# Roots as logarithm and exponential on ScalarE, spreads, scores and gate parts moved, one low split on VectorE

## What is computed

```
# first block
h = rms_norm(x, norm1_g); proj = h @ w_in            # q, k, v, glu_a, glu_b
q, k = rms_norm(q per head), rms_norm(k per head)    # root over 64 columns
log_one_minus = where(mask, log_sigmoid(-z), 0)      # z = q.k / 8, 8 heads
weights = where(mask, exp(log_sigmoid(z) + reversed exclusive cumsum(log_one_minus)), 0)
c = causal_depthwise_conv(glu_a * sigmoid(glu_b), 31 taps)
c = silu(layer_norm(c))                              # root over 512 channels
x = x + concat(weights @ v, c) @ w_out               # then a gated feed-forward
# second block
branch a: differential attention, 4 heads, o = rms_norm(o) * 0.8     # root per head
branch b: compressed + selected + window attention, 8 heads, gated
x = x + (sigmoid gates * branches) @ w_out           # gates = h @ w (16 tiles)
x = x + cross_attention(x, mem); x = rms_norm(x + peer(x))   # 16384 experts
```

## Time and profile before

| | |
|---|---|
| median of 3 runs | 2403.93 us (2403.37 to 2405.93) |
| profiled execution | 2401.27 us, span 2399.5 us, mean clock 0.997 |
| busy share | PE 98%, DVE 74%, ACT 47%, POOL 57% |
| chain that ended last | PE 88%, DVE 5%, POOL 2%, DMA 2%, ACT 2% |

### The profile page before, as it was taken

One profiled execution on the slowest core, in us unless ns is written; L12 is line 12 of the kernel. 1 busy time (PEld: TensorE's weight loads), 2 busy tenths in 40 slices (PEclk: granted clock), 3 DMA queues, 4 the chain that ended last, 5 costly groups with the idle time before them and its releaser, 6 DMA issues.

```text
span 2399.5 us, 32826 instructions
## 1 busy us (share of the span) xinstructions
PE 2345.9 (98%) x11991; PEld 1989.8 (83%) x11991; DVE 1770.4 (74%) x2989; ACT 1120.0 (47%) x2163; POOL 1370.6 (57%) x698
## 2 busy tenths in 40 slices
PE   8999999999999999999999999999999999999998
PEld 7866888888886666888889999999999888888887
DVE  4986674253236766564899978999983799999998
ACT  4356322223214556335543448888883433333333
POOL 3423455454432211433535777777777889888884
PEclk9999999999999999999999999999999999999999
DMA  4201222322421101222215687999999899999995
GB/s 161 88 18 36 100 93 81 112 88 87 178 89 53 38 34 54 105 106 95 99 62 161 226 288 261 354 351 351 354 353 383 323 360 378 376 364 358 361 356 210
DMA packets 152500, 476.60 MB, mean 199 GB/s; under 512 B 14768, under 2 KB 47920, under 8 KB 142000
## 3 DMA queue, kind: packets, MB, share of 16 engines
q1 hardware_dynamic: 115504, 340.69, 39.3%
q0 software_dynamic: 36864, 134.23, 15.6%
HBM read 422.44 MB, written 52.43 MB: 198 GB/s over the span
## 4 chain that ended last, share of the span: by engine, by line
PE 88%; DVE 5%; POOL 2%; DMA 2%; ACT 2%; issue 1%; SPq 0%; ACTq 0%; DVEq 0%; POOLq 0%
PE bank_pair L2401 22%; PE bank_pair L286 17%; PE bank_pair L288 17%; PE bank_pair L287 17%; PE bank_pair L2370 2%; PE bank_pair L775 1%; PE bank_pair L1448 1%; PE bank_pair L1485 1%; POOL u_lo L2074 1%; PE bank_pair L1501 1%; PE bank_pair L297 1%; PE bank_pair L1457 1%; PE bank_pair L298 1%; DVE stage L2545 1%; POOL w_lo L255 1%
## 5 line engine op out<-in xcount | busy, mean ns | idle before, releaser
L255 POOL TENSOR_TENSOR w_lo<-w_raw,w_hi 128x2048 fp32r<-128x2048 f32 (+3 forms) x94 | 408.9, 4350 | 573.3 <-ACT w_hi L250 573.3
L2074 POOL TENSOR_TENSOR u_lo<-u_raw,u_hi 128x1024 fp32r<-128x1024 f32 x128 | 315.8, 2468 | 168.7 <-ACT u_hi L2070 168.1
L286 PE MATMUL bank_pair<-uh,u_lo 128*128 128x384 f32 x1024 | 345.7, 338 | 6.6 <-POOL u_lo L2074 5.9
L287 PE MATMUL bank_pair<-ul,u_hi 128*128 128x384 f32 x1024 | 343.3, 335 | 0.0
L288 PE MATMUL bank_pair<-uh,u_hi 128*128 128x384 f32 x1024 | 343.2, 335 | 0.0
L2130 POOL TENSOR_TENSOR v_lo<-v_raw,v_hi 128x1024 fp32r<-128x1024 f32 x128 | 308.8, 2413 | 44.1 <-ACT v_hi L2126 42.8
L250 ACT ACTIVATE w_hi<-w_raw 128x2048 fp32r<-128x2048 f32 (+3 forms) x95 | 171.5, 1805 | 288.0 <-PE bank_pair L288 280.1
L2597 DVE TENSOR_TENSOR h_raw<-h_raw,g_in 128x384 f32<-128x384 f32 x128 | 261.0, 2039 | 49.5 <-DMA h_raw<-h_scratch 49.5
L2126 ACT ACTIVATE v_hi<-v_raw 128x1024 fp32r<-128x1024 f32 x128 | 135.8, 1061 | 288.3 <-PE bank_pair L2401 217.4
L286 PE MATMUL bank_pair<-xh,w_lo 128*128 128x512 f32 x624 | 246.0, 394 | 5.1 <-DVE sig L1737 2.1
L287 PE MATMUL bank_pair<-xl,w_hi 128*128 128x512 f32 x624 | 243.6, 390 | 0.0
(11 more groups left out here) (460 smaller groups left out, 5247.7 us busy)
## 6 DMA issues: line engine op xcount, KB each, us to landing
w_raw<-w_small SPq DMA_DIRECT2D x77, 1024.0 KB, 4.8
u_raw<-expert_u SPq DMA_DIRECT2D x128, 512.0 KB, 5.9
v_raw<-expert_v SPq DMA_DIRECT2D x128, 512.0 KB, 7.5
h_scratch<-h_act SPq DMA_DIRECT2D x128, 192.0 KB, 4.5
g_scratch<-stage SPq DMA_DIRECT2D x24, 1024.0 KB, 8.1
g_in<-g_scratch SPq DMA_DIRECT2D x16, 1536.0 KB, 11.7
h_raw<-h_scratch SPq DMA_DIRECT2D x128, 192.0 KB, 6.6
w_raw<-w_small SPq DMA_DIRECT2D x8, 768.0 KB, 4.2
```

The lines of the kernel that those rows point to most:

```text
L255: pool.tensor_tensor(wl[g % 2][:, :n], raw[g % 2][:, :n], wh[g % 2][:, :n].bitcast(F32), ALU.subtract).then_inc(sem("lo_done"), 1)
L286: pe.matmul(out, al, bh, start=(k == 0), stop=False)
L287: pe.matmul(out, ah, bl, start=False, stop=False)
L2074: pool.tensor_tensor(u_lo[c % 2][:, :, :], u_raw[c % 4][:, :, :], u_hi[c % 2][:, :, :].bitcast(F32), ALU.subtract)\
```

## The change

- The low split of weight block 1 goes from GpSimd to VectorE. The spread of the first norm goes from behind tile 3 of `in_fm` to before the sixth k (k = 5) of tile 3.
- The three places with Sqrt on ScalarE and a reciprocal of 128x512 on VectorE (q and k, layer norm, four heads of the second block) become Ln and Exp with scale -0.5, both on ScalarE.
- In `in_v` the spreads are behind tiles 2, 3, 4, 6, `scores(0)` behind tile 5, and `softplus(0)` stands before the last four convolution steps.
- Four gates parts go from steps 44 to 47 to steps 48 to 50. The high split of the next gates block goes behind the squares, and `gates_out(10)` before the eight subtractions.

```diff
-        def linear_pe(pe, name, pairs_of, ncols, ready=None, between=None, behind=(), sliced=False):
+        def linear_pe(pe, name, pairs_of, ncols, ready=None, between=None, behind=(), sliced=False, inside=()):
...
+                        hook = ready if first else dict(inside).get(n) if first_step else None
+                        products(pe, out, pairs_of(s % 2, m), hook).then_inc(sem("lin_done"), 1)
...
-        CONV_A, CONV_V = 6, (2, 0, 0, 2, 2, 2, 4, 4)
+        CONV_A, CONV_V = 6, (2, 2, 0, 0, 2, 2, 4, 4)
-        SPREAD_TILES = (3, 4, 5, 6)
+        SPREAD_TILES = (2, 3, 4, 6)
...
+            act.preload_act_table_set("natural_log_exp_and_others")
             act.wait_ge(sem("qk_sum"), 1)
-            act.activation(std16[:, :], att_bank[0][:, :], ACT.Sqrt, bias=eps[:, 0:1], scale=1.0 / HD)\
+            act.activation(std16[:, :], att_bank[0][:, :], ACT.Ln, bias=eps[:, 0:1], scale=1.0 / HD)\
                .then_inc(sem("qk_std"), 1)
-            act.preload_act_table_set("natural_log_exp_and_others")
+            act.wait_ge(sem("qk_std"), 1)
+            act.activation(rstd16[:, :], std16[:, :], ACT.Exp, scale=-0.5).then_inc(sem("qk_rstd"), 1)
...
-            act.activation(ln_std[:, :], att_bank[3][:, :], ACT.Sqrt, bias=eps[:, 0:1], scale=1.0 / CW)\
+            act.activation(ln_std[:, :], att_bank[3][:, :], ACT.Ln, bias=eps[:, 0:1], scale=1.0 / CW)\
                .then_inc(sem("ln_std"), 1)
+            act.wait_ge(sem("ln_std"), 1)
+            act.activation(ln_rstd[:, :], ln_std[:, :], ACT.Exp, scale=-0.5).then_inc(sem("ln_std"), 1)
...
-            pool.wait_ge(sem("lo_done"), 3)
-            for b in range(1, second):
+            pool.wait_ge(sem("lo_done"), 4)
+            for b in range(2, second):
...
+            def spread_at_fifth(k):
+                if k == 5:
+                    norm_spread("n1", norm_diag1, S)(pe)
+
             linear_pe(pe, "in_fm", weights_first("in_fm", xh, xl), S, follow_lo(pe, "n1"),
-                      behind=(None, first_sum, norm_spread("n1", norm_diag1, S)), sliced=True)
+                      behind=(None, first_sum), sliced=True, inside=((3, spread_at_fifth),))
...
-                    pe.wait_ge(sem("qk_rstd"), 1)
+                    pe.wait_ge(sem("qk_rstd"), 2)
...
-            in_v_behind[6] = first_scores
+            in_v_behind[5] = first_scores
+            in_v_behind[6] = last_spreads
...
+            split_lo(dve, 1)
...
-                                    row_in_group[:, 0:4].unsqueeze(2).to_broadcast([P, 4, HD]))
-                    dve.wait_ge(sem("qk_std"), 1)
-                    dve.reciprocal(rstd16[:, :], std16[:, :]).then_inc(sem("qk_rstd"), 1)
+                                    row_in_group[:, 0:4].unsqueeze(2).to_broadcast([P, 4, HD])).then_inc(sem("qk_rstd"), 1)
...
+                if n == 7:
+                    softplus(0)
...
-            dve.wait_ge(sem("ln_std"), 1)
-            chain.link(dve.reciprocal(ln_rstd[:, :], ln_std[:, :]))
+            dve.wait_ge(sem("ln_std"), 2)
...
+        HELD = (1, 1, 1, 1, 2, 1, 1)
...
+            if u < N_A:
+                return range(u, u + 1)
+            first = N_A + 2 * min(u - N_A, NU - 4 - N_A) + sum(HELD[:max(0, u - (NU - 4))])
+            return range(first, first + (2 if u < NU - 4 else HELD[u - (NU - 4)]))
...
+            for n in gates_ended(NU + 2):
+                split_hi(act, GATES["block"] + n // 2 + 2)
+            act.preload_act_table_set("natural_log_exp_and_others")
             for h in range(DA_H):
                 act.wait_ge(sem("sub_sum"), h + 1)
-                act.activation(sub_std[:, h, :], att_bank[h][:, :], ACT.Sqrt, bias=eps[:, 0:1], scale=1.0 / P)\
+                act.activation(sub_std[:, h, :], att_bank[h][:, :], ACT.Ln, bias=eps[:, 0:1], scale=1.0 / P)\
                    .then_inc(sem("sub_std"), 1)
+            for h in range(DA_H):
+                act.wait_ge(sem("sub_std"), h + 1)
+                act.activation(sub_std[:, h, :], sub_std[:, h, :], ACT.Exp, scale=-0.5).then_inc(sem("sub_std"), 1)
...
-            wait(pe, ("at_max", 2 * NU), ("bank_free", 4 + GATES["tile"] + EARLY))
+            wait(pe, ("at_max", 2 * NU))
             for h in range(DA_H):
+                if h >= 2:
+                    pe.wait_ge(sem("bank_free"), 4 + GATES["tile"] + EARLY - 2 + h - 1)
...
-                dve.wait_ge(sem("sub_std"), h + 1)
-                chain.link(dve.reciprocal(sub_std[:, h, :], sub_std[:, h, :]))
+                dve.wait_ge(sem("sub_std"), DA_H + h + 1)
                 dve.scalar_tensor_tensor(out=oab[:, h, :], in0=oab[:, h, :], scalar=subln_g[:, 0:1],
                                          in1=sub_std[:, h, :], op0=ALU.mult, op1=ALU.mult).then_inc(sem("sub_y"), 1)
+                if h == DA_H - 1:
+                    gates_out(EARLY)
```

More of the change, by code:

```diff
@@ L327, in step @@
                         first = first_step and n == 0
-                        products(pe, out, pairs_of(s % 2, m), ready if first else None).then_inc(sem("lin_done"), 1)
+                        hook = ready if first else dict(inside).get(n) if first_step else None
+                        products(pe, out, pairs_of(s % 2, m), hook).then_inc(sem("lin_done"), 1)
                         if between:
@@ L821, in first_scores, with last_spreads @@
                 scores(0)
+            def last_spreads(pe):
                 pe.wait_ge(sem("bank_free"), 4 + LAYER["in_v"]["tile"] + 6)
@@ L921, in block1_dve, with softplus @@
                 conv += CONV_A
+            def softplus(h):
+                dve.wait_ge(sem("st_ln"), h + 1)
+                if h >= 2:
+                    dve.wait_ge(sem("st_tail"), h - 1)
+                for b, (off, w) in enumerate(PIECES):
+                    ins = dve.scalar_tensor_tensor(out=soft[h % 2][:, off:off + w], in0=head_banks(h)[b][:, :w], scalar=0.0,
+                                                   in1=ln1[:, off:off + w], op0=ALU.max, op1=ALU.add)
+                ins.then_inc(sem("st_soft"), 1)
             for n in range(8):
@@ L940, in block1_dve @@
                 conv += CONV_V[n]
-            def softplus(h):
-                dve.wait_ge(sem("st_ln"), h + 1)
-                if h >= 2:
-                    dve.wait_ge(sem("st_tail"), h - 1)
-                for b, (off, w) in enumerate(PIECES):
-                    ins = dve.scalar_tensor_tensor(out=soft[h % 2][:, off:off + w], in0=head_banks(h)[b][:, :w], scalar=0.0,
-                                                   in1=ln1[:, off:off + w], op0=ALU.max, op1=ALU.add)
-                ins.then_inc(sem("st_soft"), 1)
-            softplus(0)
             softplus(1)
@@ L1160, in gates_bank @@
             return att_bank[2 + n % 2] if n < EARLY else lin_bank[n % 4]
+        HELD = (1, 1, 1, 1, 2, 1, 1)
         def gates_parts(u):
-            return range(u, u + 1) if u < N_A else range(N_A + 2 * (u - N_A), N_A + 2 * (u - N_A) + 2)
+            if u < N_A:
+                return range(u, u + 1)
+            first = N_A + 2 * min(u - N_A, NU - 4 - N_A) + sum(HELD[:max(0, u - (NU - 4))])
+            return range(first, first + (2 if u < NU - 4 else HELD[u - (NU - 4)]))
         def gates_ended(u):
-            return [q // KD for q in gates_parts(u) if q % KD == KD - 1] if u < NU else []
-        assert N_A == 2 * KD and gates_parts(NU - 1)[-1] == EARLY * KD - 1
+            return [q // KD for q in gates_parts(u) if q % KD == KD - 1] if u < NU + 3 else []
+        assert N_A == 2 * KD and gates_parts(NU + 2)[-1] == EARLY * KD - 1
         def score_bank(u, c):
@@ L1513, in block2_pe @@
                         scores(s)
-                    gates_part(gates_parts(s)[0])
+                gates_part(gates_parts(s)[0])
                 if s in (1, 2):
@@ L1518, in block2_pe @@
                     transposes(s - 2)
-                if s < NU:
-                    for q in gates_parts(s)[1:]:
-                        gates_part(q)
+                for q in gates_parts(s)[1:]:
+                    gates_part(q)
                 if s >= 3:
                     values(s - 3)
-            wait(pe, ("at_max", 2 * NU), ("bank_free", 4 + GATES["tile"] + EARLY))
+            wait(pe, ("at_max", 2 * NU))
             for h in range(DA_H):
+                if h >= 2:
+                    pe.wait_ge(sem("bank_free"), 4 + GATES["tile"] + EARLY - 2 + h - 1)
                 pe.wait_ge(sem("sub_sq"), h + 1)
@@ L1765, in block2_dve @@
                    .then_inc(sem("oab_lo"), 1)
-            for n in range(EARLY, 2 * KD):
+            for n in range(EARLY + 1, 2 * KD):
                 gates_out(n)
```

## The result

The changed kernel takes 2388.72 us (median of 4 runs, 2388.01 to 2389.31), the kernel before in the same comparison 2404.93 (2403.37 to 2408.59). The ratio is 0.9934, 95% interval 0.9921 to 0.9946. The forecast was 2389.3, range 2385.5 to 2395, 14.6 us under 2403.93. The profiled execution took 2389.23 us with a span of 2387.5, that is 12.0 us less than the profiled one of before, where the medians differ by 16.2. The 4 us between the two lie in how single executions scatter: the profiled one of before is 3.7 us under its median, the profiled one of the changed kernel 0.5 above its own.

The account below looks back on a forecast made before the run. TensorE, busy 98% of the span, was taken as the bound, with 53.6 us idle to win from. Terms 3.2 + 4.3 + 2.4 + 0.9 + 3.8 = 14.6 us off 2403.93 gave 2389.3 us, range 2385.5 to 2395.

Parts of the forecast that it names:

- Start: in_fm: waits of 1.56 and 1.51 us at tiles 2 and 4 go, 3.2 us (bounds 2.4 and 3.4).
- Heads: in_v and first heads: earlier `softplus(0)` removes the tails' wait and low clock, scores(2) 4.3 us earlier (2.7 to 5.5).
- Layer norm: out1: Ln and Exp remove waits of 1.40 and 0.75 us and two restarts, 2.4 us (bounds 1.2 and 2.6).
- Rival 4: Layer norm: table switch costs ScalarE its load twice, Silu 1.28 us later, time 2390.0 us; chance 0.10.
- Drain: End of second block's attention: moved gates parts fill the 0.63 us idle, 0.9 us (bounds -0.5 and 1.8).
- Gates tile 14: Second block: wait of 2.05 us for `gates_out(10)` and low clock behind it go, 3.8 us (bounds 2.0 and 3.9).
- Clock: Behind the first tails' wait and gates tile 14, the lower granted clock goes, 1.7 us each.
- Rival 1: Clock or handovers give less: without both clock terms 11.2 us gained, 2392.7 us; chance 0.15.
- Rivals 2 and 3: Expert stages: 2, gain lost there again, 2399 to 2404 us, chance 0.06; 3, slower from split waits, 2415, chance 0.03.

Follow-up runs that it names:

- e1: The kernel before with only the start's edits (low split of block 1 on VectorE, spread before k = 5 of tile 3): 2399.7 us, ratio 0.9983.
- e2: The changed kernel with the start, layer norm, four roots and place of `gates_out(10)` as before: 2401.25 us, ratio 0.9990.
- e6: The changed kernel with `softplus(0)` behind the last four convolution steps again: 2394.14 us.
- e3: The kernel before with Ln and Exp in the layer norm alone, no reciprocal there: 2400.57 us, ratio 0.9987.
- e5: The changed kernel with `gates_out(10)` behind the eight subtractions again, Ln and Exp kept: 2388.13 us.
- e4: The kernel before with only `gates_out(10)` moved ahead of the eight subtractions, Sqrt and reciprocals kept: 2406.18 us, ratio 1.0010.
- e7: The changed kernel run again unaltered, with its own profile: 2388.96 us.
- e12: The changed kernel with the second block's four Sqrt and four reciprocals back, order and gate parts kept: 2397.64 us, ratio 0.9975.
- e11: Unaltered repeat of e8: 2386.86 us.
- e8: The changed kernel with the second block's four sums of squares behind gates tile 10 instead of before it: 2385.84 us.
- e9: The kernel of e8 with ten matmuls nobody reads ahead of the first table of the experts: 2386.12 us.
- e10: The kernel of e9 with two and three more matmuls nobody reads before scores(2) and scores(3): 2385.35 us.

## Why the prediction was right

Step by step, forecast and measured (profile, milestones above):

- **Start, 3.2 us**: 3.5, and 3.6 by itself in e1. Both steps held, the subtraction at 2.29 us (forecast 2.3), the diagonal with 0.7 us to spare. The 0.4 us over the two waits are more than the 0.1 that the sum had for restarts.
- **Heads, 4.3 us**: 4.8, and 4.6 in e2. The sum had left out 0.2 us that TensorE waited for `rstd16`, a wait that is gone. The mechanism is shown by e6, which gives back the wait and the clock behind it. What limits now is `pre(1)` and `weights_out(0)`, as forecast.
- **Layer norm, 2.4 us**: 2.6, and 2.7 in e3's time. Rival 4 is out: Silu started 0.02 us after the load. The Trainium skill, "ScalarE: Activation LUTs", what ACT_TABLE_LOAD costs, adds a drain of some 1380 ns to each switch; the rows show none on either side of the load, and the measurement decides.
- **Drain, 0.9 us**: 0.6. The wait of 0.63 went, the other two stayed. The part isn't free by itself: e2 shows that with reciprocals on VectorE it costs 4 us, which the sum had not seen: it moved the high split ahead of the roots and did not ask which VectorE product would then meet GpSimd's split. The whole change hides it, by the Exp.
- **Gates tile 14, 3.8 us**: 4.0. The forecast named both edits as if they paid together. The runs part them: the Exp alone holds all but 0.3 us (e5), the order alone gives nothing (e4). The forecast had looked at ScalarE's copies and sigmoids for slack, found them covered, and did not ask what the same list does when the reciprocals stay. Of its terms, 1.7 us of clock were in part luck of one profile: the same wait of 2.0 us stands in e1 and e3, with no fall behind it.
- **Clock.** The two falls of before went as forecast, but the forecast priced them as if they belonged to their waits. One came back at another place (149.7, and 140 to 146 in e7), 1.5 us. Forecast to the branch layer 14.6, measured 14.1, with 0.25 of it the input's arrival: the clock took what the start and the heads gave more. These are single profiles. Over all runs of the experiments, the mean granted clock is 0.9960 in the kernel before (56 runs) and 0.9977 in the changed one (nine, with the four of the result); 0.0017 x 2400 is, as an estimate, 4 us less lost to the low clock, where the forecast had 3.4. So the size of the clock's part was right in the mean, and its places were not: which wait is followed by a fall changes from run to run.
- **Behind the branch layer** nothing was forecast. The profiles' shift of 14.1 holds to the experts, then 2 us go. The same stretch, from the branch layer to the end, is 1432.4 us in the kernel before, 1434.5 in the changed one, 1434.0 in its repeat and 1433.3 in e5, whose programs are alike there; over all twelve profiles without fills in that stretch it is 1432.4 to 1437.6, with no one place for the difference. It is scatter of single profiles; the clock's falls there, 1.7 to 5.1 us ahead of the last microseconds, are a part of it. The median of before is 2402.5 to 2404.9 in the four comparisons, that of the changed kernel 2388.7 and 2389.0: between 13.6 and 16.2 us, and 14.6 lies within.

Rival 1 (the clock gives less) happened in part in the one profile, 1.5 of its 3.4 us; the mean clock of all runs speaks against it. Rivals 2 and 3 are out: the wait for the experts' low splits is 6.4 us in 7 pieces, against 5.9 in 7.

What stays open: why a fall comes behind one wait of 0.8 to 2.1 us and not behind the next. Single profiles can't tell.

## What to carry to other kernels

Where one engine is busy 98% of the time, go through its waits one by one, price each with what would be late next, and add the low clock behind it where a row shows one, as a mean over runs and not as a fixed price. All five terms came within 0.5 us of what their stretch showed, and the clock that came back at another place, 1.5 us, was in none of them. Ask also what the next wait has in reserve: the 1.4 us ahead of the branch layer bounded what the order alone could win. A reciprocal of 128x512 on the engine that empties banks costs 3.35 us, and the larger price is in the lists of other engines that follow it: look a layer further on than the wait that is removed. Edits that look separate can need each other; undo each in the full change and run each alone, since the two answers differ (e4 and e5).

## What the runs showed of the hardware

- The clock's falls are partly chance, and waits feed them. In single profiles, counted up to 975 us: before 2, e1 3, e3 3, e4 4, with all or most of the old waits; e2 1, e6 1, e12 2; the changed kernel and the variants that keep all its edits of the stage or add to them (after, e5, e7 to e11) 1, 1, 1, 1, 1, 1 and 0. By the length of TensorE's wait, a fall during it or up to 3 us behind its end:

| wait | us | profiles that have it | with a fall |
|---|---|---|---|
| first table of the experts | 4.0 | 12 | 12 |
| first tails, old order | 3.1 | 5 | 5 |
| tile 14 in e2, branch layer in e4 and e12 | 6.1, 2.5, 4.9 | 3 | 3 |
| tile 14 (before, e1, e3) | 2.0 | 3 | 1 |
| tile 2 of in_fm (before, e2, e3, e4) | 1.6 to 2.2 | 4 | 1 (e3, 2.2) |
| first square of the second block | 1.4 | 10 | 2 |
| two waits near 765 to 778 us | 1.2, 1.0 | 14 | 6 |
| scores(2) and scores(3), new order, no fill | 0.8, 1.1 | 8 | 4 |

  In these rows every wait of 2.5 us or more had a fall, and of the shorter ones some; waits of 1.3 to 1.5 us at tile 4 of in_fm, in out1 and near 1365 to 1380 us had none in any profile. It is no rule: in e8 a wait of 3.4 us in the expert stages, at 1827 us, had none either. No edit touches the code near 765 to 778 us. Most falls lost 1.7 us by the windows; five of the 22 up to 975 us were twice as long (one in e2, e4 and e12, two in e3), up to 3.4 us. They are a large part of what single executions of this kernel scatter.
- Cutting a wait of 4.0 us to 1.8 with matmuls nobody reads kept the clock at 2.4 GHz in e9 and e10; in the twelve other profiles it fell there (before, after, e1 to e8, e11, e12).
- A table switch on ScalarE took 1.28 us from end to end, with 0.01 us between the load and a Silu that was ready (e3), and 0.02 between Exp and load.
